# Keys of the second layer by seven half-sized block products per unit, with their norm made as sums

## The reference

```
layer 0:  x += diff_attention(rope(rms(h @ w_qkv)), caches) @ w_o      h = rms_norm(x, norm_mix_g[0])
          x += (silu(g) * u) @ w_down                                  g, u = rms_norm(x, norm_ffn_g[0]) @ w_gate_up
shared:   kv = rms_norm(x, kv_norm_g) @ w_kv_s                         k = kv[:, :1024], v = kv[:, 1024:]   (outputs too)
layer 1:  x += stick_breaking(rms_norm(x, norm_mix_g[1]) @ w_q, k, v, caches) @ w_o
          x += swiglu(rms_norm(x, norm_ffn_g[1]))
```

## Time and profile before

| what | value |
|---|---|
| median of 3 runs | 1640.53 us (1640.08 to 1642.52) |
| the profiled execution | 1639.72 us, its span 1637.9 us |
| TensorE busy | 1616.6 us, 99% |
| VectorE busy | 1132.0 us, 69% |
| ScalarE busy | 722.5 us, 44% |
| GpSimd busy | 151.9 us, 9% |
| granted TensorE clock | 1.00 |
| DMA | 267.54 MB, mean 163 GB/s |

### The profile page before, as it was taken

How to read it: one execution, slowest core, us unless ns; L and a number is a source line. 1 busy time by engine, 2 the same in 40 slices (tenths; PEclk the granted TensorE clock), 3 DMA queues, 4 the chain that set the end, 5 groups by cost and what they waited for, 6 DMA issues and landing times.

```text
span 1637.9 us, 31443 instructions
## 1 busy us (share of the span) xinstructions
PE 1616.6 (99%) x13180; PEld 1486.7 (91%) x13180; DVE 1132.0 (69%) x1576; ACT 722.5 (44%) x1196; POOL 151.9 (9%) x132
## 2 busy tenths in 40 slices
PE   9999999999999999999999999999999999999999
PEld 8888766699999999999999897766999999999999
DVE  5765477678984797488742337877689748964874
ACT  6444476765551344134432214666555413531441
POOL 0000000012210011011000100000122101110110
PEclk9999999999999999999999999999999999999999
DMA  7133899931222122222243458997422221221222
GB/s 288 64 113 139 348 420 419 419 151 52 87 95 104 52 78 103 78 69 87 103 150 136 168 210 350 419 419 325 167 78 78 104 78 55 101 104 52 78 104 90
DMA packets 40252, 267.54 MB, mean 163 GB/s; under 512 B 4400, under 2 KB 4784, under 8 KB 10928
## 3 DMA queue, kind: packets, MB, share of 16 engines
q1 hardware_dynamic: 36720, 252.95, 40.2%
q0 software_dynamic: 3392, 12.58, 2.2%
HBM read 249.79 MB, written 15.73 MB: 162 GB/s over the span
## 4 chain that ended last, share of the span: by engine, by line
PE 86%; DMA 5%; DVE 5%; issue 2%; ACT 2%; SPq 0%; DVEq 0%; ACTq 0%
PE ps L584 30%; PE ps L799 29%; PE ps L268 4%; PE ps L270 4%; PE ps L269 4%; DMA kv<-in_v_s 3%; PE ps L1264 2%; PE ps L1323 2%; DVE s_lo L748 2%; PE ps L1205 2%; PE ps L611 2%; PE ps L1242 1%; DMA kv<-in_v_a 1%; DMA xT<-in_v_a 1%; PE ps L1227 1%
## 5 line engine op out<-in xcount | busy, mean ns | idle before, releaser
L230 ACT ACTIVATE w_hi<-w_raw 128x2048 fp32r<-128x2048 f32 x55 | 105.0, 1909 | 189.8 <-PE ps L584 158.5
L246 DVE TENSOR_TENSOR w_lo<-w_raw,w_hi 128x2048 fp32r<-128x2048 f32 x55 | 126.0, 2292 | 71.7 <-ACT w_hi L230 71.7
L744 ACT ACTIVATE s_hi<-t 128x512 fp32r<-128x512 f32 x176 | 109.4, 626 | 144.5 <-PE ps L799 65.5
L799 PE MATMUL ps<-hs_hi,s_hi 128*128 128x320 f32 x528 | 163.8, 310 | 0.0
L799 PE MATMUL ps<-hs_lo,s_hi 128*128 128x320 f32 x528 | 163.2, 309 | 0.0
L799 PE MATMUL ps<-hs_hi,s_lo 128*128 128x320 f32 x528 | 163.2, 309 | 0.0
L584 PE MATMUL ps<-gu_hi,w_hi 128*128 128x320 f32 x692 | 157.8, 309 | 0.2
L584 PE MATMUL ps<-gu_lo,w_hi 128*128 128x320 f32 x692 | 157.7, 309 | 0.0
L584 PE MATMUL ps<-gu_hi,w_lo 128*128 128x320 f32 x692 | 157.7, 309 | 0.0
L748 DVE TENSOR_TENSOR s_lo<-t,s_hi 128x512 fp32r<-128x512 f32 x176 | 133.0, 762 | 5.3 <-ACT s_hi L744 4.5
L657 DVE TENSOR_TENSOR sg<-ps,rows 128x640 f32<-128x640 f32 x47 | 38.7, 823 | 128.5 <-PE ps L584 128.5
(11 more groups left out here) (302 smaller groups left out, 3968.2 us busy)
## 6 DMA issues: line engine op xcount, KB each, us to landing
w_raw<-in_w SPq DMA_DIRECT2D x99, 1024.0 KB, 4.8
kv<-in_k_a SPq DMA_DIRECT2D x12, 1024.0 KB, 17.7
...
```

Of the source, the lines that this page charges most:

```text
L230: nc.scalar.activation(w_hi[s][:, :, :], w_raw[:, s, :, :], ACT.Copy).then_inc(hi_done, 1)
L246: nc.vector.tensor_tensor(w_lo[s][:, :, :], w_raw[:, s, :, :], w_hi[s][:, :, :].bitcast(F32), ALU.subtract).then_inc(lo_done, 1)
L744: nc.scalar.activation(s_hi[i][:, :, :], factor(j % 2, i), ACT.Copy).then_inc(hi_done, 1)
L799: last = nc.tensor.matmul(ps[:, bank[i], 0:HALF], w[:, p, :], m[:, p, :], start=(i < 3 and p == 0 and a == 0), stop=(p == 3 and a == 2), s ...
```

## The change

The keys are made by `gu_unit`, in four units of seven block products, from weights laid out in blocks on the host (`blocks_of`), as gate and up are. The norm `kv` becomes a `PairNorm`: its hooks run in `d02` in place of the plain norm's, with the squares in a buffer of their own (`sq2_k`) and with one slot of `sg` for the scaled tile. During `d02`'s last unit the first four factors of the keys' first unit are made instead of one whole split. The keys' evictions are `ks_dve`, `ks_act` and `ks_pool`; GpSimd multiplies most of them by the row. The values still read the plain `h_hi` and a plain low part, which now lies in `mix_lo`: both are made in the keys' last unit (`v_hi`, `v_lo`), as soon as the block sums that lie in the same memory have been read. The high part of the next layer's input moves from beside the keys to behind them, into `h_lo`.

```diff
-        order = [("qkv", 12, TT, 1), ("oa", 4, 2, 1), *layer(0), ("ks", 4, 2, 1), ("vs", 4, TT, 1), ("qb", 4, 2, 1),
+        order = [("qkv", 12, TT, 1), ("oa", 4, 2, 1), *layer(0), ("ks", KU, 0, 7), ("vs", 4, TT, 1), ("qb", 4, 2, 1),
...
-                nc.scalar.activation(sq2[:, t % 2, :], xT[:, t, :], ACT.Square).then_inc(mix["sq"], 1)
+                nc.scalar.activation(self.squares[:, t % 2, :], xT[:, t, :], ACT.Square).then_inc(mix["sq"], 1)
...
                     if ch is not None:
-                        ch.link(nc.vector.tensor_tensor(halves(sg[:, n, :]), y, halves(rstd_row), ALU.mult))
-                        y = halves(sg[:, n, :])
+                        scaled = halves(sg[:, 0 if one_slot else n, :])
+                        ch.link(nc.vector.tensor_tensor(scaled, y, halves(rstd_row), ALU.mult))
+                        y = scaled
                     nc.vector.tensor_tensor(x, y, x, ALU.add).then_inc(x_done, 1)
                     hook(dve, j, n)
-        def whole_act(norm, x0):
-
-            def hook(act, j):
...
-        def whole_dve(norm):
-
...
-        def pair_act(f):
-
-            nm = norms[f"ffn{f}"]
-            return lambda act, j: nm.pair_act(act, j, (lambda: copy_p1(act, f * N_F, 0)) if j == 3 else None)
+        def pair_act(name, v):
+
+            return lambda act, j: norms[name].pair_act(act, j, (lambda: copy_p1(act, v, 0)) if j == 3 else None)
...
-                    residual_act(act, d, lambda a: split_hi(a, d, 4, 0), hook, (prod, 7 * (v + n)))
+                    residual_act(act, d, after, hook, (prod, 7 * (v + n)))
+
+        def norm_pool(pool, nm):
+            for p in range(4):
+                nm.difference(pool, p)
+                nm.add(pool, 2 * p)
+                nm.add(pool, 2 * p + 1)
 
...
+        V_TILES = (6, 7, 0, 1, 2, 3, 4, 5)
+        ks_last = 7 * (N_F + KU - 1)
+        v_free = {6: 1, 7: 1, 0: 2, 1: 2, 2: 3, 3: 3, 4: 6, 5: 6}
+
+        def v_hi(act, i):
+            t = V_TILES[i]
+            act.wait_ge(prod, ks_last + v_free[t])
+            nc.scalar.activation(h_hi[:, t, :], xT[:, t, :], ACT.Copy, scale=norms["kv"].g(t)).then_inc(norm["hi"], 1)
+
+        def v_lo(dve, i):
+            t = V_TILES[i]
+            dve.wait_ge(norm["hi"], KT + i + 1)
+            nc.vector.scalar_tensor_tensor(mix_lo[:, t, :], xT[:, t, :], norms["kv"].g(t), h_hi[:, t, :].bitcast(F32),
+                                           ALU.mult, ALU.subtract).then_inc(norm["lo"], 1)
+
+        def ks_pe(pe, nm):
+            for j in range(KU):
+                gu_unit(pe, "ks", j, N_F + j, nm if j == 0 else None)
+
+        def ks_act(act, nm):
+            gu_hi_block(act, "ks", 0, 4)
+            nm.square(act, KT - 1)
+            gu_hi_block(act, "ks", 0, 5)
+            gu_hi_block(act, "ks", 0, 6)
+            copy_p5(act, N_F, 0)
+            for i in range(6):
+                gu_hi_block(act, "ks", 1, i)
+            nc.scalar.preload_act_table_set("natural_log_exp_and_others")
+            nm.root(act, 6)
+            gu_hi_block(act, "ks", 1, 6)
+            for j in range(1, KU - 1):
+                copy_p1(act, N_F + j, j % 2)
+                gu_hi_block(act, "ks", j + 1, 0)
+                gu_hi_block(act, "ks", j + 1, 1)
+                copy_p5(act, N_F + j, j % 2)
+                for i in range(2, 7):
+                    gu_hi_block(act, "ks", j + 1, i)
+            copy_p1(act, N_F + KU - 1, 1)
+            for i in range(4):
+                v_hi(act, i)
+            copy_p5(act, N_F + KU - 1, 1)
+            for i in (4, 5):
+                v_hi(act, i)
+            split_hi(act, "vs", 0, 0, (prod, ks_last + 4))
+            for i in (6, 7):
+                v_hi(act, i)
+            split_hi(act, "vs", 1, 1, (prod, ks_last + 7))
+            for t in range(KT):
+                nc.scalar.activation(h_lo[:, t, :], xT[:, t, :], ACT.Copy, scale=nm.g(t, G_MIX1)).then_inc(mix1["hi"], 1)
+
+        def ks_pool(pool, nm):
+
+            def scaled(x, t):
+                nc.gpsimd.tensor_tensor(qkp[:, t, HALF:SEQ], x[:, 0:SEQ - HALF], rstd_row[:, HALF:SEQ], ALU.mult)
+                return nc.gpsimd.tensor_tensor(qks[:, t, :], x[:, SEQ - HALF:HALF], rstd_row[:, SEQ:TOK], ALU.mult)
+
+            norm_pool(pool, nm)
+            for j in range(KU):
+                v, s, t = N_F + j, j % 2, KT + 2 * j
+                if j == 0:
+                    pool.wait_ge(*nm.rooted)
+                pool.wait_ge(ff["u3"], v + 1)
+                pool.wait_ge(ff["p5"], v + 1)
+                nc.gpsimd.tensor_tensor(up_k[:, s, HALF:TOK], up_k[:, s, HALF:TOK], p5_k[:, s, :], ALU.add)\
+                    .then_inc(ff["c22"], 1)
+                pool.wait_ge(ff["c22"], v + 1)
+                scaled(up_k[:, s, HALF:TOK], t + 1)
+                pool.wait_ge(ff["c12"], v + 1)
+                nc.gpsimd.tensor_tensor(qkp[:, t + 1, 0:HALF], up_k[:, s, 0:HALF], rstd_row[:, 0:HALF], ALU.mult)
+                pool.wait_ge(ff["c21"], v + 1)
+                scaled(c21_k[:, s, :], t).then_inc(kq["kev"], 1)
+
+        def ks_dve(dve, nm):
+
+            def u2(j):
+                v, s = N_F + j, j % 2
+                dve.wait_ge(prod, 7 * v + 2)
+                dve.wait_ge(ff["p1"], v + 1)
+                if j > 1:
+                    dve.wait_ge(kq["kev"], j - 1)
+                nc.vector.tensor_tensor(up_k[:, s, 0:HALF], ps[:, 3 * s + 1, 0:HALF], p1_k[:, s, :], ALU.add)\
+                    .then_inc(ff["u2"], 1)
...
+            def lo(j, *blocks):
+                for i in blocks:
+                    gu_lo_block(dve, "ks", j, i)
+
+            lo(0, 4)
+            u2(0)
+            sum4(dve, "ks", 0)
+            lo(0, 5, 6)
...
+            u2(3)
+            for i in range(4):
+                v_lo(dve, i)
+            g0(3)
+            for i in (4, 5):
+                v_lo(dve, i)
+            u3(3)
+            split_lo(dve, "vs", 0, 0)
+            c12(3)
+            for i in (6, 7):
+                v_lo(dve, i)
+            c21(3)
...
-        norms = {"mix0": Norm(G_MIX0, 0, col_n=0), "ffn0": PairNorm(G_FFN0, 0, 0, 0),
-                 "kv": Norm(G_KV, 1, row_n=1, col_n=1), "ffn1": PairNorm(G_FFN1, 1, 2, KT * 4)}
+        norms = {"mix0": Norm(G_MIX0, 0, col_n=0), "ffn0": PairNorm(G_FFN0, 0, 0),
+                 "kv": PairNorm(G_KV, 1, KT * 3, col_n=1, squares=sq2_k), "ffn1": PairNorm(G_FFN1, 2, KT * 4)}
...
-            pool.wait_ge(kq["kev"], KT)
+            ks_pool(pool, norms["kv"])
+            pool.wait_ge(kq["kev"], KU)
+            pool.wait_ge(ff["g0"], N_F + KU)
...
-            residual_act(act, "oa", lambda a: first_his(a, "g00", range(4)), pair_act(0))
-            ffn_act(act, 0, norms["ffn0"], whole_act(norms["kv"], X_F0 - KT))
-            for j in range(4):
-                split_hi(act, "ks", j + 1, 1 - j % 2)
-                if j == 0:
-                    nc.scalar.preload_act_table_set("natural_log_exp_and_others")
-                    norms["kv"].root(act, 4)
-                    act.wait_ge(norm["cols"], 4)
-                for t in range(2 * j, 2 * j + 2):
-                    nc.scalar.activation(h2_hi[:, t, :], xT[:, t, :], ACT.Copy, scale=norms["kv"].g(t, G_MIX1))\
-                        .then_inc(mix1["hi"], 1)
-
+            residual_act(act, "oa", lambda a: first_his(a, "g00", range(4)), pair_act("ffn0", 0))
+            ffn_act(act, 0, norms["ffn0"], pair_act("kv", N_F), lambda a: first_his(a, "ks", range(4)))
+            ks_act(act, norms["kv"])
+            act.wait_ge(norm["cols"], 4)
...
-            ffn_dve(dve, ch, 0, norms["ffn0"], whole_dve(norms["kv"]))
-            kq_dve(dve, "ks", kq["kev"], KT, 1.0, False, rooted=norms["kv"].rooted)
+            ffn_dve(dve, ch, 0, norms["ffn0"], pair_dve(norms["kv"]), lambda e: first_los(e, "ks", range(4)))
+            ks_dve(dve, norms["kv"])
...
-                nc.vector.scalar_tensor_tensor(h_lo[:, t, :], xT[:, t, :], norms["kv"].g(t, G_MIX1),
-                                               h2_hi[:, t, :].bitcast(F32), ALU.mult, ALU.subtract)\
+                nc.vector.scalar_tensor_tensor(mix_lo[:, t, :], xT[:, t, :], norms["kv"].g(t, G_MIX1),
+                                               h_lo[:, t, :].bitcast(F32), ALU.mult, ALU.subtract)\
                     .then_inc(mix1["lo"], 1)
...
-            kq_pe(pe, "ks", kq["kev"], h_hi, h_lo, norms["kv"].ready, mid=lambda: norms["kv"].pe(pe, 4))
+            ks_pe(pe, norms["kv"])
+            banks_free = [(ff["g0"], N_F + 3), (ff["c21"], N_F + 3), (ff["c12"], N_F + 3), (ff["g0"], N_F + 4),
+                          (ff["c21"], N_F + 4)]
             for j in range(4):
+                if j < 2:
+                    pe.wait_ge(norm["lo"], (KT + 6, KT + 8)[j])
+                if j == 1:
+                    pe.wait_ge(kq["kev"], KU)
                 token_unit(pe, "vs", j, kq["vev"], k_done=mix1["free"] if j == 3 else None,
```

(12 more changed lines are left out.)

180 lines of the change are left out of this document (122 added, 58 removed).

## The result

The changed kernel takes 1651.1 us (median of 6 runs, 1650.55 to 1653.6) against 1641.41 us (6 runs) for the kernel before on the same chip: ratio 1.0061, 95% interval 1.0048 to 1.0074. It is slower by 9.7 us; 1648 was forecast, with a range to 1652.5. The profiled execution took 1651.73 us (span 1649.9). In the profiles the second layer's values start at 889.54 us instead of 881.06, +8.5 against the +7.8 of the sum.

The account below looks back on a forecast made before the run. TensorE, busy 99% of the span, was taken as the bound; 14.8 us of idle less 7.04 of matmuls gave +7.8 (+7.4 to the keys' end, +0.4 at the values), so 1648 us, range 1642.5 to 1652.5.

Parts of the forecast that it names:

- The 48 matmuls: In the keys, TensorE does 336 matmuls instead of 4 units of 96, a gain of 7.04 us.
- The loop of 13.55: In d02, VectorE and ScalarE need 13.55 us per unit against TensorE's 10.56, 3.0 us too long.
- The contention: In d02, GpSimd's adds delay VectorE's odd-tile adds by 0.75 us, three times, with bounds 0 and 1.38 each.
- The path: From d02's first split to the keys' end: hs done at 842.9, keys end at 888.4 instead of 881.06, +7.4 us.
- TensorE's waits of 1.5 and 3.7: In d02, TensorE idles 1.5 us before its third unit and 3.7 before its fourth, waiting for x.
- the term that was too small: In the keys' units, GpSimd's longer share costs VectorE some; taken as nothing, bounds 0 to 3 us.
- the 0.4 at the start of the values: In the last keys unit VectorE's work ends at 12.7 us against TensorE's 12.32: +0.4, between 0 and 2.
- The clock: Rival: TensorE's clock falls to 1.2 GHz for one unit's 84 matmuls after long idle, costing 12.3 us, about 1660; 5%.
- Behind the values: After the values' start nothing else is due before its time, so no further term was added.
- the preparation hides: Rival in d02: the loop comes under 10.56 us, giving -4.9 us, 1635.6, or 1633.5 with everything hidden; 8%.
- late but shorter: Rival: no contention on adds or weight sums and less ScalarE wait per loop, +2.5 to +4, about 1643.5; 11%.
- the delay vanishes in the second attention: Rival: waits for cached values in the second attention absorb what the keys cost, 1640.5 to 1641; 4%.

Follow-up runs that it names:

- e1b: Changed kernel without making the second layer's sums, differences and low parts of x for the keys; 1636.15 us, -5.6 against the kernel before.
- e4: Changed kernel with the same VectorE and ScalarE instructions in another order behind the first layer's last down projection; +5.0 us against the kernel before.
- e2: Changed kernel with GpSimd's seven adds of the keys' squares over 32 of 640 columns; +4.2 us against the kernel before.
- e3: Changed kernel with 45 extra unread matmuls filling TensorE's waits in d02 and the keys' first product; +7.1 us against the kernel before.
- e5: Kernel before with 58 extra unread matmuls (8.5 us) ahead of the second layer's values; +12.5 us against the kernel before.

## Why the prediction was right

Of the 3.1 us between 1648 and 1651.1, 0.7 are in the values' start and 1.2 behind it, 0.9 are the kernel before (1641.41 in this comparison, 1640.53 in the prediction's), and 0.3 were rounded off 1648.3. Work, loop, lock and path came as said; the clock and the second attention did not.

- *The 48 matmuls.* Priced at 7.04; without the preparation 6.5 of it arrives at the values and 5.6 at the end (e1b).
- *The loop of 13.55.* Measured 13.43 without contention (799.00 - 785.57), 14.22 with it; 13.55 + 0.75 = 14.30 was said. Timing the loop behind the first output projection, adding the two products and holding it against 10.56 gave the sign. That the order and not only the work made it so long is e4's addition: the same instructions took 11.1, and 12.7 where GpSimd's adds met two of them.
- *The contention.* 0.75 was chosen between 0 and 1.38; 1.60, 1.58 and 1.59 for 0.82 make it 0.76 to 0.78. VectorE's add ends 0.69 us after GpSimd's (807.42 against 806.73), where the prediction said about 0.7. The rule of the Trainium skill that it weighed (SBUF — State Buffer, "SBUF: two separate sides") is borne out: the add, with two SBUF operands, does not get on beside GpSimd's. By that rule 0.75 was due in full, and e2 gives back the 3.6 us.
- *The path.* Third split at 813.3, measured 813.22; last low part of hs at 842.9, measured 842.60; TensorE's waits of 1.5 and 3.7, measured 1.35 and 3.43. From hs to the end of the keys 45.5 was said and 46.9 measured. That is the term that was too small, by 1.4, where the prediction had put nothing, with bounds of 0 to 3. From the starts of the units, 851.55, 864.08 and 877.22, 0.4 of it is in what was left of the first, 0.2 in the second (12.53 for 12.32) and 0.8 in the third (13.14), most of that at the wait for an eviction by VectorE shown below. The fourth took 12.32, and the 0.4 at the start of the values did not come. d02 ended at 829.4 and not at 827.8: that is the slower clock, and it only shortened the wait for ha.

```profile
871.87 0.39 PE L803 MATMUL ps<-hd_hi,s_hi 128*128 128x320 f32 x1 [0.59 <-DVE up_k L1994]
```

- *The clock.* Here the prediction was wrong, though not in its number. It gave the fall 5%, priced it at 12.3 us for a unit at half speed, and said that it would be wrong with a clock under 1.00. The clock did fall, for 3 to 4 us and twice. It cost 3.3 us of TensorE and nothing of the path up to the values, since VectorE was the last (e3); that the range held in spite of it is luck, as far as the prediction goes. The rule of the Trainium skill (TensorE: Matmul & The Clock Gate, "Why this matters for your kernels") agrees with the falls behind the waits of 3.43 and 3.31 us. The missing step was to ask who is last while the clock is down.
- *Behind the values.* The sum stopped at their start and carried the delay to the end one for one. e5 shows that this holds only by chance: 8.5 us there became 12.5. In the changed kernel +8.5 became +9.7; the 12.0 of its profile is held against a fast execution of the kernel before (above). The forecast's 1648 lacks this term, 1.2 us by the medians; e3's -1.3 and e5's +4.0 say that it could have had either sign.

The rival that the preparation hides is refuted by e1b against the changed kernel, *late but shorter* by the odd adds, and *the delay vanishes in the second attention* by its opposite.
